# Attention over a prompt: when Pool scales a head's keys, where ScalarE copies outputs, and how two kinds of PSUM banks are dealt out

## The reference

```python
q = _rmsnorm(concat([q_nope, q_pe]), q_norm_g)         # per head
k = _rmsnorm(concat([k_nope, k_rot]), k_norm_g)        # per head; k_rot is shared by the heads
s = einsum('bqhd,bkhd->bhqk', q, k) * 96 ** -0.5
s = where(kpos <= qpos, s, -inf)
out = einsum('bhqk,bkhd->bqhd', softmax(s), v)
```

## Time and profile before

| | us |
|---|---|
| median of 3 runs | 2058.05 (2055.15 to 2059.5) |
| the profiled execution, its own time | 2060.78 |
| its span in the trace | 2059.0 |
| PE busy in the span | 1935.3 (94%) |
| DVE busy | 981.8 (48%) |
| ACT busy | 750.4 (36%) |
| POOL busy | 561.1 (27%) |

### The profile page before, as it was taken

How to read it: one execution, slowest core, us unless ns; L and a number is a source line. 1 busy time by engine, 2 the same in 40 slices (tenths; PEclk the granted TensorE clock), 3 DMA queues, 4 the chain that set the end, 5 groups by cost and what they waited for, 6 DMA issues and landing times. The chain is left out here.

```text
span 2059.0 us, 36182 instructions
## 1 busy us (share of the span) xinstructions
PE 1935.3 (94%) x12672; PEld 1826.8 (89%) x12672; DVE 981.8 (48%) x1591; ACT 750.4 (36%) x1556; POOL 561.1 (27%) x552
## 2 busy tenths in 40 slices
PE   6999997888869999999999699999999999999997
PEld 5999996566649999999998399999999999999997
DVE  6124135688547777777777642323232222223132
ACT  5111224566536666676766332111111111111011
POOL 3232233777710000100000354222222223121221
PEclk8999998999969999999999599999999999999999
DMA  6122000000032222222222111020202111120202
GB/s 218 42 75 63 11 15 14 1 0 0 1 90 63 75 72 72 74 72 75 75 69 109 41 41 53 14 70 21 61 25 56 51 31 52 34 76 6 75 15 100
DMA packets 180603, 108.47 MB, mean 53 GB/s; under 512 B 52132, under 2 KB 177154, under 8 KB 180276
## 3 DMA queue, kind: packets, MB, share of 16 engines
q1 hardware_dynamic: 180358, 107.21, 18.2%
q10 hardware_dynamic: 174, 0.30, 0.1%
HBM read 97.47 MB, written 10.00 MB: 52 GB/s over the span
## 5 line engine op out<-in xcount | busy, mean ns | idle before, releaser
L1911 PE MATMUL banks<-comb_hi,pageT_hi 128*128 128x272 f32 x1024 | 234.1, 310 | 0.0
L1801 DVE TENSOR_REDUCE k_sums<-k_sq 128x8 f32<-128x512 f32 x256 | 174.4, 681 | 91.9 <-ACT k_sq L1619 91.9
L2268 DVE TENSOR_TENSOR xT<-xT,banks 128x1074 f32<-128x1074 f32 x64 | 81.6, 1274 | 276.7 <-PE banks L244 276.7
L1911 PE MATMUL banks<-comb_hi,pageT_lo 128*128 128x272 f32 x1024 | 212.4, 289 | 0.0
L1911 PE MATMUL banks<-comb_lo,pageT_hi 128*128 128x272 f32 x1024 | 212.0, 288 | 0.0
L1619 ACT ACTIVATE k_sq<-banks 128x512 f32<-128x512 f32 x256 | 152.1, 594 | 141.9 <-PE banks L1911 139.0
L233 POOL TENSOR_TENSOR w_down_lo<-w_down_raw,w_down_hi 128x512 fp32r<-128x512 f32 x64 | 95.0, 1484 | 346.6 <-ACT w_down_hi L229 346.6
L2150 ACT ACTIVATE a_hi<-relu 128x1074 fp32r<-128x1074 f32 x32 | 35.4, 1105 | 396.0 <-DVE relu L2256 396.0
L233 POOL TENSOR_TENSOR w_out_up_lo<-w_out_up_raw,w_out_up_hi 128x1024 fp32r<-128x1024 f32 x40 | 101.8, 2554 | 273.7 <-ACT w_out_up_hi L229 273.7
L244 PE MATMUL banks<-hf_hi,w_out_up_hi 128*128 128x358 f32 x768 | 169.5, 329 | 0.0
L244 PE MATMUL banks<-a_hi,w_down_lo 128*128 128x358 f32 x768 | 169.1, 328 | 0.0
(11 more groups left out here) (382 smaller groups left out, 4078.5 us busy)
## 6 DMA issues: line engine op xcount, KB each, us to landing
page_latents<-in_cache_kv_latent SPq DMA_DIRECT2D x256, 128.0 KB, 2.1
w_out_up_raw<-in_w_up SPq DMA_DIRECT2D x32, 512.0 KB, 4.2
w_down_raw<-in_w_down SPq DMA_DIRECT2D x64, 256.0 KB, 2.7
w_in_raw<-in_w_in SPq DMA_DIRECT2D x17, 512.0 KB, 3.9
x_spill<-xT SPq DMA_DIRECT2D x1, 4296.0 KB, 15.0
xT<-x_spill SPq DMA_DIRECT2D x1, 4296.0 KB, 13.9
page_ropes<-in_cache_k_rope SPq DMA_DIRECT2D x256, 16.0 KB, 1.7
w_out_up_raw<-in_w_o SPq DMA_DIRECT2D x8, 512.0 KB, 4.4
```

Of the source, the lines that this page charges most:

```text
L1801: nc.vector.tensor_reduce(ksum[par][:, j, :], sq[j % 2][:, :].rearrange("p (h c) -> p h c", h=H), AX_X, ALU.add)\
L1911: mm = pe.matmul(banks[:, 2 * (j % 2) + half, 0:WC], x[j % AHEAD][:, k, :], w[par][:, k, half, :], start=k == 0 and a == 0, stop=k == KL - ...
L2268: nc.vector.tensor_add(x, x, slot(s)[:, :, 0:TB]).then_inc(down.evacuated[s], 1)
```

## The change

In POOL's stream `prepare_k` moves from the end of loop n (for head n+3) to go 0 of the next loop, behind `shift(., ., 1)` and `diagonal(., 1)`, and gets a wait for the units of the head before. In ACT's stream `keep_output` of the second chunk is written at the end of loop n instead of the start of loop n+1. The five units alternate between banks 5 and 7, and PE waits before unit u for DVE's read of unit u-2. The scores alternate between banks 0 and 1, and PE waits before block j for the copy of block j-2.

```diff
-    SCORE_BANKS = (0, 1, 5)
-    SPREAD_BANK, TURN_BANK, UNIT_BANK = 4, 6, 7
+    SPREAD_BANK, TURN_BANK = 4, 6
+
+    def unit_bank(par, u):
+        return (5, 7)[(par + u) % 2]
...
             def prepare_k(n):
+                ge(pool, s["unit_transposed"], n * NU)
                 nc.gpsimd.tensor_mul(kh[:, :, 0:NOPE], ...
...
                     prepare_q(1)
-                    prepare_k(1)
                 for go in range(GOES):
                     if have(n, 0) and go < GOES - 1:
                         shift(n, par, go + 1)
                     if have(n, 0) and go < 2:
                         diagonal(n, 1 + go)
+                    if have(n, 2) and go == 0:
+                        prepare_k(n + 2)
...
                     if have(n, 1) and go == 5:
                         shift(n + 1, 1 - par, 0)
-                    if have(n, 3) and go == 5:
-                        prepare_k(n + 3)
...
-                act.copy(S[par][:, start_of[j]:start_of[j] + width[j]], banks[:, SCORE_BANKS[j % 3], 0:width[j]])...
+                act.copy(S[par][:, start_of[j]:start_of[j] + width[j]], banks[:, j % 2, 0:width[j]])...
...
                 for go in range(GOES):
-                    if have(n, -1) and go == 0:
-                        keep_output(n - 1, 1 - par, before, 1)
                     if have(n, 1):
                         keep_scores(n + 1, 1 - par, 2 * go)
...
                     if have(n, 2) and go < NU:
-                        split_hi(n + 2, par, go)
+                        split_hi(n + 2, par, go, unit_bank(par, go))
...
                     if go == GOES - 1 and have(n, 1):
                         probabilities(n + 1, 1 - par, 0)
+                    if go == GOES - 1 and have(n, 0):
+                        keep_output(n, par, pair, 1)
                 if isinstance(n, int) and n == H - 1:
-                    keep_output(n, par, pair, 1)
                     keep_output(n, par, pair, 2)
...
-                        split_lo(n + 2, par, go)
+                        split_lo(n + 2, par, go, unit_bank(par, go))
...
-            def transpose_unit(n, u, bank=UNIT_BANK):
-                if bank == UNIT_BANK:
-                    ge(pe, s["unit_lo_done"], n * NU + u)
+            def transpose_unit(n, u, bank, first=False):
+                if not first:
+                    ge(pe, s["unit_lo_done"], n * NU + (u - 1))
...
-                ge(pe, s["copied"], n * NB + (j - 2))
-                bank = SCORE_BANKS[j % 3]
+                ge(pe, s["copied"], n * NB + (j - 1))
+                bank = j % 2
...
-                        transpose_unit(n + 2, go)
+                        transpose_unit(n + 2, go, unit_bank(par, go))
```

More of the change, by code:

```diff
@@ L1131, in _, with split_hi @@
             act.wait_ge(s["gain_done"], 1)
-            def split_hi(n, par, u, bank=UNIT_BANK):
+            def split_hi(n, par, u, bank):
                 act.wait_ge(s["unit_transposed"], n * NU + (u + 1))
@@ L1147, in keep_scores @@
                 ge(act, s["pv_done"], n * NB - 2 * NB + (j + 1))
-                act.copy(S[par][:, start_of[j]:start_of[j] + width[j]], banks[:, SCORE_BANKS[j % 3], 0:width[j]]).then_inc(s["copied"], 1)
+                act.copy(S[par][:, start_of[j]:start_of[j] + width[j]], banks[:, j % 2, 0:width[j]]).then_inc(s["copied"], 1)
             def keep_spread(n, par, c):
@@ L1208, in _, with split_lo @@
             v.wait_ge(s["gain_done"], 1)
-            def split_lo(n, par, u, bank=UNIT_BANK):
+            def split_lo(n, par, u, bank):
                 last = u == NU - 1
@@ L1374, in loop @@
                     for u in range(NU):
-                        transpose_unit(0, u, 2 + u)
+                        transpose_unit(0, u, 2 + u, first=True)
                 for go in range(GOES):
```

## The result

| | before | after |
|---|---|---|
| median of 8 runs, us | 2058.24 (2054.65 to 2059.79) | 2062.97 (2061.11 to 2065.74) |
| the profiled execution: own time, span | 2060.78, 2059.0 | 2065.74, 2064.0 |
| PE starts the next phase (its first product with `w_ukv`), us from the span's start | 578.06 | 581.46 |

What follows compares the result with a forecast made beforehand. Each loop was taken as a chain through several engines, none full. Terms -7.1 (units), 0 (scores), 0 (output copies) and +0.1 (key scaling) made -7.0 us: 2051.0 us from a median of 2058.05, range 2044.0 to 2057.5.

Steps and rivals of the forecast that it cites:

- the key scaling of POOL: POOL's two scaling instructions, 1.9 us, moved to go 0: +0.1 us over loops 0 to 5, bounds -4 and +4.4.
- rival 2: POOL's run without a gap shuts DVE's maximum out in four more loops, 3.7 us each: 2065.8 us; chance 0.09.
- Units in two banks: PE's waits at the unit transposes for DVE's read of the one unit bank go: -7.1 us, bounds 0 and 14.0.
- the smaller of two things: A loop gains the lesser of PE's removed wait and DVE's standing time before its first maximum of chunk two.
- Scores in two banks: PE waits for the copy of block j-2, with 0.7 us to spare at the tightest place: cost 0, at most 3.6 us.
- Output copies of ACT: ACT's queue keeps its order, so PE's 14.0 us of waits for ACT stay: cost 0, between -0.1 and +0.1.
- Rival 4: Output copies really come later than the score copies, so PE's first values wait longer; chance next to nothing.
- The exponential: ACT's exponential, delayed by the moved scaling, may make PE wait up to 0.5 us in loops 2 and 4.
- Rival 1: DVE is late in other loops too, one more maximum hindered per loop, +4.4 us: 2055.3 us; chance 0.27.
- Rival 3: With less idle, PE keeps clock 1.00 in loops 1, 3 and 4; 3.6 us more gained, 2047.4 us; chance 0.10.
- The border between the two parts of a loop: DVE's first maximum of chunk two, in go 4; from it to the next head's first values a fixed chain, 10.2 us.
- signs for "wrong": Maxima of 3 us and more in several loops, DVE not standing before that maximum, or PE waiting for copied scores.

Runs made afterwards that it cites:

- e1_k_back: The changed kernel with POOL's key scaling put back at the end of the loop, all else as changed: 2052.18 us, 0.9975 of the kernel before.
- e9_banks_only: Both bank changes alone (also called "two banks"), key scaling and ACT's output copy placed as in the kernel before: 2051.27 us, 0.9968 of the kernel before.
- e2_k_moved_only: The kernel before with only POOL's key scaling moved as in the change, one unit bank kept: 2080.19 us, 1.0106 of the kernel before.
- e11_later_maximum: The changed kernel, with DVE waiting at score block 4 for ACT's copy of block 5 too: 2065.88 us, 1.0039 of the kernel before.
- e3_pool_gap: The changed kernel, with POOL waiting in go 2 until DVE's maximum of score block 4 is done: 2052.73 us, 0.997 of the kernel before.

## Why the prediction was wrong, step by step

**The step that failed is the key scaling of POOL**: +0.1 us, with bounds of -4 and +4.4. Measured, it is +10.8 us in this kernel (against e1_k_back; +11.7 against e9_banks_only, which also has ACT's old order) and +21.6 with one unit bank. The loops show where: against "two banks" after is longer by 2.8 us in loop 0, 3.9 in loop 3 and 2.7 in loop 5, the three loops in which the long maximum is new; that is 9.4 of 11.5 us in the seven loops (by the rows before rounding). The rest lies in loops 1, 2 and 4.

The working went wrong in one sentence: "The next diagonal takes the delay up, as POOL stood 1.94 us before it." Two things are wrong in it. The 1.94 us are of loop 4, and the prediction took them for all six loops; in loops 0, 3 and 5 the wait was 0.85 us, less than the 1.9 of the scaling, so there the scaling used it up. And the idle time was put down as slack that costs nothing to fill, while DVE's maximum behind it came through where POOL had waited and stood where POOL had not. The row that says so was in hand: the one long maximum of the earlier trace rows lay in the one loop in which POOL came to that diagonal without a wait (the row at 397.46 above, which the prediction does not use). I took the hit for chance, and as evidence against rival 2 I noted that loops 2 and 3 have the same order of work. The same order with a wait of POOL in it is another case.

The upper bound failed for the same reason: it was built from the mild row (1.31 for 0.58), and the 5.66 beside it went into the text ("a price from 0 over 0.7 to 5.1 us") but not into the bound. The mild row was no milder kind of event: it ended at 479.27 (477.96 + 1.31), 0.43 us after POOL stopped at 478.84 (476.82 + 2.02 in the earlier trace rows, with 0.98 us of idle behind it). DVE stood until POOL stopped in both rows, and only POOL's stop came sooner in one.

**Rival 2** was what happened, and nearly at its price. It had four more hits at 3.7 us each, with 2065.8 us; three more came, at 3.1 us on average (9.4 by 3). Three at 3.7 would have given 2051.0 + 11.1 = 2062.1; the measurement is 2062.97. Its chance of 0.09 was the error, not its mechanism. That the price fits is in part luck: the 3.7 was read from the kernel with one unit bank, and there the new long maxima cost more (e2_k_moved_only: loops 0, 3 and 5 longer by 6.2, 5.9 and 7.5 us).

**Units in two banks**, -7.1 us: right in sum. Measured alone with the two score banks, which cost nothing, it is -7.6. By loops it is less exact, and that the sum fits is in part luck, as misses on both sides cancel: loop 1 gains 4.2 us (31.0 to 26.8, forecast 3.5) though its long maximum stays, loop 2 nothing (28.0 and 28.2, forecast 0), loop 3 gains 2.7 (forecast 1.0), loop 4 1.4 (0.9), and loop 5 loses 0.5 (forecast a gain of 0.5). Loop 3 gained more than the 0.97 us that PE had waited there, so the rule "the smaller of two things" does not hold loop by loop. In after this gain is larger, 17.2 us (2080.19 less 2062.97), since the second bank also spares PE part of the wait behind each long maximum.

**Scores in two banks**, 0: right (0.9999). **Output copies of ACT**, 0: right as far as the runs can tell (PE's wait 14.0 us before, 13.7 after; e1_k_back and e9_banks_only differ by less than their intervals). Rival 4, that the copies come later than before, did not happen.

**The exponential**, "a new wait of up to 0.5 us in loops 2 and 4": it came in more loops and larger (5.5 us in seven waits, the longest 1.1). The kernel with the pause has 4.8 of it and is as fast as the one without the moved scaling, so it costs little.

**The other rivals.** Rival 1 (one more maximum hindered a little in each loop) was the mild form of what came. Rival 3 (a higher clock) did not come. Loops 1 to 4 of after by stretch (columns as in the earlier trace rows, the granted clock is the first number after POOL's):

```profile
388.50:416.30 27.80, 22.63 (x128) 17.13 (x128) 20.98 (x27) 16.43 (x33) 20.34 (x25) 1.00 0.01 1
416.30:445.10 28.80, 25.36 (x128) 19.32 (x127) 25.65 (x34) 16.64 (x33) 21.65 (x25) 0.88 0.00 1
445.10:473.50 28.40, 24.90 (x124) 18.74 (x123) 21.30 (x29) 16.76 (x33) 20.13 (x25) 0.88 0.00 0
473.50:502.30 28.80, 22.81 (x132) 17.42 (x130) 24.06 (x32) 16.12 (x33) 21.60 (x25) 1.00 0.00 0
```

Loops 1 and 4 have 1.00 where they had 0.94 in the earlier trace rows, loops 2 and 3 have 0.88 where they had 1.00 and 0.94; loops 2 and 4, with the same work, last 28.8 us each at 0.88 and at 1.00, so the length of a loop does not follow this clock.

**The signs named beforehand.** The border between the two parts of a loop held nearly: from DVE's first maximum of chunk two to the next values it was to stay 10.2 us, and is 9.3 to 10.2 in loops 0 to 5 of after (9.4 in loop 0, 383.00 to 392.42). Two of the three signs for "wrong" were there: long maxima in several loops, and DVE no longer standing before that maximum. The third, PE waiting for a copied score, was not.

## What to carry to other kernels

Before you fill an engine's idle time, ask what gets through in it: a wait of 1 or 2 us on an engine off the critical path may be what lets another engine through (here 0.85 to 1.94 us of POOL). A single odd row, ten times as long as its like, is a case with a condition; look for what is different in that loop before you call it chance. And a wait put in on purpose, on the engine that has time, can be worth as much as taking one out (here 10.2 us).

## What the runs showed of the hardware

A DVE `tensor_tensor` with both inputs in SBUF can stand behind POOL for many POOL instructions, not one. In loop 0 of after a maximum that takes 0.56 us at 381.92 took 6.84 at 373.47, across the rest of one shift, a second one (1.97 for both), a scaling of 1.14 and six shifts more, and ended 0.44 us after POOL stopped; in the loop of the earlier trace rows this distance was 0.43 us, in e11_later_maximum 0.43. No semaphore holds DVE there: the wait lies inside the instruction, so engines do not wait for each other through semaphores alone. While DVE is shut out POOL runs at its full pace (1.97 for two shifts); where DVE gets through, both are slower: 2.54 for the two shifts, and in DVE's group of four the last three, which took 1.09 in loop 0 (7.93 less 6.84), take most of the 3.79. The Trainium skill, SBUF — State Buffer, Who interferes with whom, says that such a DVE instruction contends with a GpSimd one that reads SBUF, and that the shared port pair is an exclusive lock; that the one that issues first holds it for its whole instruction it says there of DVE's 2-port modes. The contention is what the traces show too. That the wait ends with the instruction in progress they show in some rows (the 1.31 of the earlier trace rows, the 1.43 at 365.45) and not in these: the longest of POOL's instructions there takes 1.14 us, and DVE stood more than 6.

What decides between the two is shown as a condition at one place, not as a mechanism: block 4's maximum was shut out 21 of 21 times after a diagonal to which POOL came without a wait, 0 of 33 times after one for which it had waited, and the moment at which DVE comes did not decide it. DVE's own idle time parts the same cases and is not ruled out. A pause of 0.5 us while DVE stands ends it (e3_pool_gap). Why a wait some 1.8 us before DVE comes (the 0.85 before 428.76, and DVE at 430.52) still makes a difference stays open.
